# Gate and up weights read as chunks of 2 k-blocks x 1024 columns instead of 4 x 512

## What is computed

```python
def swiglu(h, wg, wu, wd):
    return (jax.nn.silu(h @ wg) * (h @ wu)) @ wd

def moe_swiglu(h, w_router, wg, wu, wd):
    ...
    logits = (xt @ w_router).astype(jnp.float32)
    top_v, top_i = lax.top_k(logits, TOP_K)
    gates = jax.nn.softmax(top_v, axis=-1)
    gate = jnp.sum(jax.nn.one_hot(top_i, N_EXPERTS, dtype=jnp.float32) * gates[..., None], axis=1)
    y = jnp.zeros_like(xt)
    for e in range(N_EXPERTS):
        y = y + gate[:, e:e + 1].astype(xt.dtype) * swiglu(xt, wg[e], wu[e], wd[e])
    return y.reshape(B, S, D)
```

## Time and profile before

| | us |
|---|---|
| median of 3 runs | 1585.43 |
| lowest and highest | 1585.12, 1586.38 |
| profiled execution, its own time | 1585.69 |
| its span | 1583.9 |
| of it before the first pair's first matmul | 669 |
| first pair | 669 to 894 |
| second, third and fourth pair | 894 to 1117, 1117 to 1342, 1342 to 1567 |

### The profile page before, as it was taken

One profiled execution on the slowest core, in us unless ns is written; L12 is line 12 of the kernel. 1 busy time (PEld: TensorE's weight loads), 2 busy tenths in 40 slices (PEclk: granted clock), 3 DMA queues, 4 the chain that ended last, 5 costly groups with the idle time before them and its releaser, 6 DMA issues.

```text
span 1583.9 us, 20830 instructions
## 1 busy us (share of the span) xinstructions
PE 1523.3 (96%) x7379; PEld 1259.0 (79%) x7379; DVE 1285.2 (81%) x1555; ACT 1104.4 (70%) x1475; POOL 118.7 (7%) x242
## 2 busy tenths in 40 slices
PE   6999999999999999699999999999999999999995
PEld 5788788888888888588887788788787887787784
DVE  5686585566545556689999999999999999999998
ACT  3664564645434364278888888888888888788886
POOL 3433431101000010100000000000000000000000
PEclk9999999999999999699999999999999999999998
DMA  9545444535545554369999999999999999999995
GB/s 330 202 156 173 156 158 135 182 116 186 173 146 198 193 179 160 136 230 372 391 397 406 393 385 387 387 406 407 385 386 387 391 408 400 384 387 386 399 407 224
DMA packets 203364, 462.70 MB, mean 292 GB/s; under 512 B 7934, under 2 KB 12428, under 8 KB 203132
## 3 DMA queue, kind: packets, MB, share of 16 engines
q1 hardware_dynamic: 200304, 453.80, 78.5%
q0 software_dynamic: 1904, 5.38, 1.3%
q10 hardware_dynamic: 1052, 2.19, 0.4%
HBM read 460.29 MB, written 1.05 MB: 291 GB/s over the span
## 4 chain that ended last, share of the span: by engine, by line
PE 67%; DMA 13%; DVE 12%; issue 3%; ACT 2%; DVEq 2%; SPq 0%; ACTq 0%
PE ps L2138 8%; PE ps L2139 8%; PE ps L2140 8%; DVE wlo_sb L1378 8%; DMA raw_sb<-moe_wu 7%; PE ps L2595 6%; PE ps L2597 6%; PE ps L2596 6%; PE ps L2610 5%; PE ps L2611 5%; DMA raw_sb<-moe_wg 2%; DMA raw_sb<-moe_wd 2%; ACT whi_sb L998 2%; DMA raw_sb<-w_in 2%; PE ps L2556 2%
## 5 line engine op out<-in xcount | busy, mean ns | idle before, releaser
L1378 DVE TENSOR_TENSOR wlo_sb<-raw_sb,whi_sb 128x1024 fp32r<-128x1024 f32 x662 | 772.6, 1219 | 44.8 <-ACT whi_sb L998 42.1
L998 ACT ACTIVATE whi_sb<-raw_sb 128x1024 fp32r<-128x1024 f32 x662 | 661.3, 1053 | 137.9 <-PE ps L2597 69.5
L1370 DVE TENSOR_TENSOR wlo_sb<-raw_sb,whi_sb 128x1024 fp32r<-128x1024 f32 (+2 forms) x198 | 230.1, 1203 | 146.1 <-ACT whi_sb L990 145.1
L990 ACT ACTIVATE whi_sb<-raw_sb 128x1024 fp32r<-128x1024 f32 (+2 forms) x198 | 192.3, 1023 | 163.3 <-PE ps L2140 131.8
L2138 PE MATMUL ps<-whi_sb,xlo_sb 128*128 128x512 f32 (+2 forms) x544 | 212.8, 391 | 4.4 <-DVE xlo_sb L1417 4.2
L2139 PE MATMUL ps<-wlo_sb,xhi_sb 128*128 128x512 f32 (+2 forms) x544 | 208.5, 383 | 0.0
L2140 PE MATMUL ps<-whi_sb,xhi_sb 128*128 128x512 f32 (+2 forms) x544 | 208.4, 383 | 0.0
L2595 PE MATMUL ps<-whi_sb,xlo_sb 128*128 128x512 f32 x448 | 181.5, 405 | 5.7 <-DVE wlo_sb L1378 4.4
L2610 PE MATMUL ps<-whi_sb,xhi_sb 128*128 128x512 f32 x448 | 177.8, 397 | 2.2 <-DVE wlo_sb L1378 2.1
L2597 PE MATMUL ps<-whi_sb,xhi_sb 128*128 128x512 f32 x448 | 175.4, 391 | 0.0
L2611 PE MATMUL ps<-wlo_sb,xhi_sb 128*128 128x512 f32 x448 | 175.0, 391 | 0.0
(11 more groups left out here) (394 smaller groups left out, 2129.2 us busy)
## 6 DMA issues: line engine op xcount, KB each, us to landing
raw_sb<-moe_wg SPq DMA_DIRECT2D x113, 1024.0 KB, 11.3
raw_sb<-moe_wd SPq DMA_DIRECT2D x112, 1024.0 KB, 10.9
raw_sb<-moe_wu SPq DMA_DIRECT2D x109, 1024.0 KB, 11.9
raw_sb<-w_in SPq DMA_DIRECT2D x40, 1024.0 KB, 5.2
raw_sb<-w_out SPq DMA_DIRECT2D x16, 1024.0 KB, 5.0
raw_sb<-ffn_wg SPq DMA_DIRECT2D x10, 1024.0 KB, 5.1
raw_sb<-ffn_wu SPq DMA_DIRECT2D x10, 1024.0 KB, 5.1
raw_sb<-ffn_wd SPq DMA_DIRECT2D x10, 1024.0 KB, 5.1
```

Of the source, the lines that this page charges most:

```text
L990: nc.scalar.activation(whi[i % SPLIT][:, c:c + k // 2, 0:n], raw[i % RAW][:, c:c + k // 2, 0:n], ACT.Copy).then_inc(hi_ready, 1)
L998: nc.scalar.activation(whi[i % SPLIT][:, c:c + KC // 2, :], moe_raw(i, l)[:, c:c + KC // 2, :], ACT.Copy).then_inc(hi_ready, 1)
L1370: op = V.tensor_tensor(wlo[i % SPLIT][:, c:c + k // 2, 0:n], raw[i % RAW][:, c:c + k // 2, 0:n], whi[i % SPLIT][:, c:c + k // 2, 0:n], ALU ...
L1378: op = V.tensor_tensor(wlo[i % SPLIT][:, c:c + KC // 2, :], moe_raw(i, l)[:, c:c + KC // 2, :], whi[i % SPLIT][:, c:c + KC // 2, :], ALU.s ...
```

## The change

It alters `job_chunks` and all that reads it. The 7 blocks become three groups of two blocks (1024 columns) and one single block (`GROUPS` = 4). A group is 4 gate chunks and then 4 up chunks of 2 k-blocks x 1024 columns; the seventh block stays at 4 x 512. The number of chunks, their bytes, the steps of a pair, `FIRST_ORDER` and `PAIR_ORDER` are as before.

- Gate of a group fills both banks of its job (`bank_of`), and up of the group fills the same two. The first up chunk waits for the reading of gate: for H half by half (`heavy_bank_free`), for L at once (`light_waits`). The first gate chunk of the next group waits for the reading of up.
- Within a gate or up chunk PE runs the first half of columns through and then the second (`order_of`). PE tells of the end of the first half with the new semaphore `h_half_ps`.
- ACT reads H's gate as two `Silu` of 512 columns, and DVE makes H's product as two of 512. L's reading, L's folds, `Silu`, product and splits, and H's turn and split, are done once for a group with twice the width.
- `act_h` moves into the unused half of `xlo`. `gate_l` and `value_l` become one buffer `row_l` of 1024 columns.

```diff
 def job_chunks():
-    up = [Chunk(which, p * NC, NC, k0, KC, p, k0 == 0, k0 + KC == KT)
-          for p in range(BLOCKS) for which in "gu" for k0 in range(0, KT, KC)]
+    up = [Chunk(which, q * WIDE, WIDE, k0, WIDE_K, q, k0 == 0, k0 + WIDE_K == KT)
+          for q in range(WIDE_BLOCKS) for which in "gu" for k0 in range(0, KT, WIDE_K)]
+    up += [Chunk(which, WIDE_BLOCKS * WIDE, NC, k0, KC, WIDE_BLOCKS, k0 == 0, k0 + KC == KT)
+           for which in "gu" for k0 in range(0, KT, KC)]
...
@@ scalar_program, pair; act_hi_moe(act, i + SPLIT, j) stands ahead of it in both @@
                     if i in plan.gate[HEAVY_JOB]:
-                        p = plan.gate[HEAVY_JOB][i]
-                        act.wait_ge(split_used, number(AT_MOE, i + 1, PER, j))
-                        if not first(j) or p:
-                            act.wait_ge(hT_ps, done + p)
-                        nc.scalar.activation(act_h[:, :], acc[:, HEAVY_JOB, 0, :], ACT.Silu).then_inc(hg_silu, 1)
+                        q = plan.gate[HEAVY_JOB][i]
+                        if not first(j) or q:
+                            act.wait_ge(hT_ps, done + q)
+                        for p in blocks_of(q):
+                            if p % 2 == 0 and q < WIDE_BLOCKS:
+                                act.wait_ge(h_half_ps, 2 * WIDE_BLOCKS * j + 2 * q + 1)
+                            else:
+                                act.wait_ge(split_used, number(AT_MOE, i + 1, PER, j))
+                            nc.scalar.activation(act_h_of(p), in_blocks(h_bank(p, "g")), ACT.Silu).then_inc(hg_silu, 1)
...
                     if i in plan.gate[LIGHT_JOB]:
...
-                        nc.scalar.activation(gate_l[:, :], acc[:, LIGHT_JOB, 0, :], ACT.Copy).then_inc(lg_copied, 1)
+                        nc.scalar.activation(row_l[:, 0:NC * len(blocks_of(q))], l_banks(q, "g"),
+                                             ACT.Copy).then_inc(lg_copied, 1)
...
+            def heavy_bank_free(chunk, j, h):
+
+                q = chunk.block
+                if chunk.which == "u" and chunk.n == WIDE:
+                    pe.wait_ge(hg_silu, BLOCKS * j + 2 * q + h + 1)
+                elif q:
+                    pe.wait_ge(h_act, BLOCKS * j + 2 * (q - 1) + bank_of(chunk, h) + 1)
+                elif h == 0 and not first(j):
+                    pe.wait_ge(yg_lo, 4 * j)
...
@@ light_waits @@
+                elif chunk.first and chunk.which == "u" and chunk.n == WIDE:
+                    pe.wait_ge(lg_copied, done + q + 1)
+                elif chunk.first and q:
+                    pe.wait_ge(lu_copied, done + q)
```

More of the change, by code:

```diff
@@ L434, in build @@
         ahead_in_ahi2 = sb("ahead_in_ahi2", [PART, KC, NC], stack=ahead)
-        sb("below_alo2", [PART, NC + below], stack=ahead)
+        sb("below_alo2", [PART, below], stack=ahead)
         ahead_in_alo2 = sb("ahead_in_alo2", [PART, KC, NC], stack=ahead)
@@ new lines, in pair @@
+                    if i in plan.gate[LIGHT_JOB]:
+                        q = plan.gate[LIGHT_JOB][i]
+                        act.wait_ge(split_used, number(AT_MOE, i + 1, PER, j))
+                        if not first(j) or q:
+                            act.wait_ge(luT_ps, done + q)
+                        nc.scalar.activation(row_l[:, 0:NC * len(blocks_of(q))], l_banks(q, "g"),
+                                             ACT.Copy).then_inc(lg_copied, 1)
+                    if i in plan.silu_l:
+                        q = plan.silu_l[i]
+                        act.wait_ge(lgT_ps, done + q + 1)
+                        if not first(j) or q:
+                            act.wait_ge(l_lo, done + q)
+                        nc.scalar.activation(l_act_of(q), l_tp(q, "g"), ACT.Silu).then_inc(l_silu, 1)
@@ L2590, in heavy_step @@
                         hi, lo = x_lhs(k, HEAVY_JOB)
+                        if c == 0 and chunk.first:
+                            heavy_bank_free(chunk, j, h)
                     first, last = chunk.first and c == 0, chunk.last and c == chunk.k - 1
[L2592 to L2597, removed]
+                    o = acc[:, HEAVY_JOB, bank_of(chunk, h), :]
+                    w = c * (chunk.n // NC) + h
+                    mm(o, lo, whi[i % SPLIT][:, w, :], start=first, stop=False)
+                    mm(o, hi, wlo[i % SPLIT][:, w, :], start=False, stop=False)
+                    op = mm(o, hi, whi[i % SPLIT][:, w, :], start=False, stop=last)
+                    if chunk.which != "d" and chunk.n == WIDE and last and h == 0:
+                        op.then_inc(h_half_ps, 1)
                 op.then_inc(split_used, 1)
             def light_step(i, chunk):
-                out = acc[:, LIGHT_JOB]
-                for c in range(chunk.k):
+                for c, h in order_of(chunk):
                     k = chunk.k0 + c
@@ L2606, in light_step @@
                     first, last = chunk.first and c == 0, chunk.last and c == chunk.k - 1
-                    for h in range(chunk.n // NC):
-                        o = out[:, h if chunk.which == "d" else "gu".index(chunk.which), :]
-                        w = c * (chunk.n // NC) + h
-                        mm(o, both, whi[i % SPLIT][:, w, :], start=first, stop=False)
-                        op = mm(o, both, wlo[i % SPLIT][:, w, :], start=False, stop=last)
-                op.then_inc(split_used, 1)
+                    o = acc[:, LIGHT_JOB, bank_of(chunk, h), :]
@@ new lines, in light_step @@
+                    w = c * (chunk.n // NC) + h
+                    mm(o, both, whi[i % SPLIT][:, w, :], start=first, stop=False)
+                    op = mm(o, both, wlo[i % SPLIT][:, w, :], start=False, stop=last)
+                op.then_inc(split_used, 1)
+            def heavy_bank_free(chunk, j, h):
[6 more added lines that the diff above has]
+                    pe.wait_ge(yg_lo, 4 * j)
@@ L2614, in heavy_waits @@
             def heavy_waits(chunk, j):
[L2616 removed]
                 if chunk.which == "d":
                     if chunk.first:
[L2619 to L2626 removed]
+                        pe.wait_ge(hg_silu, BLOCKS * (j + 1))
@@ L2649, in fold @@
+            def fold(q, which):
+                out = l_tp(q, which)
+                for a in range(NC * len(blocks_of(q)) // PART):
+                    at = a % (NC // PART) * LIGHT
+                    op = mm(out[:, a // (NC // PART), at:at + LIGHT], row_l[:, a * PART:(a + 1) * PART], C("fold"), start=True,
                             stop=True)
```

216 lines of the change are left out of this document (114 added, 102 removed).

## The result

The changed kernel takes 1612.4 us (median of four, 1609.1 to 1615.3) against 1585.3 us: 1.017 times as long, 95% interval 1.015 to 1.019. A second set of runs (`after_again`) gave 1609.8 against 1586.2 us, 1.015 (1.014 to 1.017). Predicted were 1598.5 us, 1583 to 1609: the direction is right, the loss is half of the real one, and the median lies outside the range. The profiled execution took 1609.1 us, 23.4 more than that of before.

A forecast was written before the change was run, and what follows sets the result against it. PE was taken as nearly as full as the DMA, so new waits cost time: 1585.7 us profiled, +9.0 in the first pair, +4.2 in three later ones, 1598.9; stated as 1598.5 us, range 1583 to 1609.

The forecast's parts named there:

- longer rows: Gate and up transfers: 192 wide chunks, each 0.147 us quicker, 28 us; only 3.0 us a later pair counted as gain.
- Step 4 of the first pair: H's turn from gate to up: PE waits 2.94 us plus 1.28 for the Silu table's load, 4.2 us.
- Step 12: First pair, H's turn at steps 11 to 12: PE waits 2.94 less a gather of 0.87, 2.1 us.
- Two H turns of a later pair: Gate to up of H: PE waits 1.1 us a turn for ACT's reading, which stands behind a copy.
- the first turn of a later pair: DVE is behind anyway and PE waits for `wlo`, so only 0.7 of 2.1 us was counted.
- L's turns: PE waits for L's reading of gate: 0.8 us a turn in later pairs, 2.5 in all in the first.
- Fewer bursts: Folds and transposes in 12 bursts a pair instead of 21, 0.12 us saved each: 1.1 us less a pair.
- ACT and DVE save some calls too; both have idle time behind PE.: On ACT and DVE: fewer calls from merged work, and idle time behind PE; no size given.
- The tail makes up 1.5 us: End of the first pair, L's steps paced by DVE: a late PE makes up 1.5 us, between 0 and 2.8.
- The clock: PE's clock falls to half behind the waits at steps 4 and 12 of the first pair: +2 to +4 us.
- costs more: Rival: rows stay at 386 GB/s (+9 us) or PE's clock falls in the new waits; 1602 to 1611 us, chance 0.20.
- GB/s near 408 in gate and up when DMA is full: Sign expected in the changed kernel's trace: gate and up transfers near 408 GB/s, with the queue held up by PE.

The follow-up runs named there:

- b_wide: The kernel before with only its gate and up transfers drawn as rows of 4 KB, computation unchanged: 1571.5 us, 0.991 of before.
- a_read_first: The changed kernel with ACT reading the accumulators before it makes the copy for step i+3: 1593.5 us, 1.004 of before.
- a_table: The changed kernel with a dummy Silu on ACT behind the copy for step 3 of the first pair, loading the table there: 1607.1 us.
- a_lumps: The changed kernel with ACT's readings first, the early table load and most of DVE's work per group left out (output not valid): 1582.6 us.
- a_narrow: The changed kernel with only its gate and up transfers drawn as rows of 2 KB, as before the change: 1608.7 us.
- a_both_narrow: The changed kernel with ACT's readings first, the early table load and gate and up transfers in rows of 2 KB: 1592.3 us.
- a_pool_s: The changed kernel with ACT's readings first, the early table load and L's subtraction moved from DVE to POOL: 1598.0 us.
- a_both: The changed kernel with ACT's readings first and the Silu table loaded early by a dummy Silu: 1591.6 us.

## Why the prediction was wrong by half

**The frame was right.** PE, not the DMA, sets the time; the 28 us of "longer rows" don't exist; what PE can gain from them was put at 3.0 us a later pair and is 3.7 to 4.2 (`b_wide`). The place of the loss, ACT's copy ahead of the reading, is confirmed by `a_read_first`: 16 to 19 us hang on it.

**Terms that held.** Step 4 of the first pair: 4.2 said, 4.3 measured, the table's load in it 1.28 and 1.42 (`a_table`). Step 12: 2.1 and 2.0. Step 28: 1.1 and 1.1. Two H turns of a later pair: 2.2 and 1.2 + 0.9. Step 8: 1.1 and 0.9. The 0.7 us put for the first turn of a later pair also came out, at steps 7 and 8, but by luck: it is not the turn (see below).

**Terms that were too high.** L's turns: 1.6 a later pair and 2.5 in the first; measured 0.75 and 0.86. In the second pair L's reading ends at the 6.4 us that I had, but H's own wait makes PE's H step end at 6.0 instead of 5.7; in the third pair the reading ends at 6.1.

**Terms that failed.**
- *Fewer bursts, -1.1 us in each pair.* It is about zero. A fold of 16 small matmuls delays PE by 1.70 us and two of 8 by 0.81 each, eight transposes 0.80 and twice four 0.70: merged bursts cost 0.08 to 0.1 us more apiece, 0.7 to 0.8 a pair, and that is what the fewer late first matmuls save. I took the one from a row and not the other. 4.4 us in all.
- *"ACT and DVE save some calls too; both have idle time behind PE."* This is the step that failed most. With 97 of 100 us busy in gate and up, DVE has no idle time that counts. Its work per group now comes in pieces twice as long: H's product makes PE wait 0.47 us three times a later pair (0.2 forecast, from the start of the product in the earlier trace rows, where the subtraction ahead of it was over earlier) and 0.4, 1.0 and 0.5 us at steps 20, 36 and 44 of the first pair, where I had nothing. Waits for `wlo` appear at steps 22 and 38, and at four steps of the first pair (1.2 us). `a_lumps` gives back 2.1 to 2.6 us a pair of it, nearly all from the waits for `wlo`. Together this is about 7 us. The sum was 10 us short (23.4 against 13.2): these 7, 4.4 for the bursts and 1.7 for the clock, less 4 that L's turns had too much.
- *The tail makes up 1.5 us.* At step 82 nothing: PE's wait is 2.8 us in both. It is no lateness of chunks but DVE adding the scattered results (2.47 us in one piece), which waits for PE's own scatter and moves with it. What does come back is 0.9 us at step 69, a wait that the prediction doesn't name.
- *The clock.* Named as a rival at +2 to +4 us and not put into the sum. Both places named, step 4 and step 12, had the fall: 3.4 us at half, 1.7 lost each time. Net of the fall of before, at the end of the pair, that is 1.7 us in the profiled execution.

**The sum again.** First pair, measured: 12.1 us of new waits in it and 0.5 ahead of the next pair's first matmul, 1.7 of clock, 1.2 in late matmuls and larger bursts, less 0.9 at step 69: 14.6. The second pair: H turns 2.15, L turns 0.75, H's product 1.4, `wlo` at steps 7 and 8 0.7, `wlo` later 0.6, late matmuls and larger bursts 0.9, less 2.6 for late chunks that no longer are and 0.3 at the scatter: 3.6.

**A fold that hid in a wait.** PE's wait at step 7 of a later pair is 1.4 us instead of 0.6 in all variants of the new computation. The second pair, ahead of step 7, before and after:

```profile
912.69 0.60 PE L2683 MATMUL ps<-con_sb,pick_sb 128*128 128x128 f32 x4
913.13 1.00 PE L2648 MATMUL ps<-con_moe_sb,gate_l_sb 128*128 128x64 f32 x8
914.67 0.50 PE L2610 MATMUL ps<-whi_sb,xhi_sb 128*128 128x512 f32 x1 [0.54 <-DVE wlo_sb L1378]
```

```profile
926.96 0.60 PE L2754 MATMUL ps<-con_sb,pick_sb 128*128 128x128 f32 x4
928.90 0.50 PE L2670 MATMUL ps<-whi_sb,xhi_sb 128*128 128x512 f32 x1 [1.34 <-DVE wlo_sb L1423]
```

Step 7 starts no later for it: step 6 is 4.84 us long in both, and in the third pair step 7 starts 21.5 us into the pair in both. Before, L's fold of block 0, 0.81 us, stood in this wait and cost nothing. Now L's first fold is due only when the group's gate is complete, at a place where PE is busy. The longer wait is the sign of work that has moved out of it.

**The rival "costs more"** (1602 to 1611) came nearest in time (1609.8 and 1612.4) and had a small part of the reason: the clock yes, the rows no. That the rows move no faster was wrong as a fact (402 GB/s), and its +9 us are not what was lost either: with short rows the changed kernel takes no longer (`a_narrow`), nor does it without the turn waits (`a_both_narrow`). That its sum comes near is luck. The sign given as proof, "GB/s near 408 in gate and up when DMA is full", could not show, for the DMA was never full.
The Trainium skill, "SBUF — State Buffer", section "SBUF: two separate sides", says that DVE with two SBUF inputs and a GpSimd instruction that reads SBUF exclude each other for a whole instruction. `a_pool_s` agrees: 1.22 us became 2.32 beside POOL's 1.54.

**What stays open.** What else stands between `a_lumps` and `b_wide`. That the wait for H's product can be shortened is not shown: in `a_lumps` it stayed. And no complete kernel here beats the one before. `b_wide` shows 13.6 us of room, but to compute what the text says it needs gate and up of a job in banks of their own at 1024 columns, four for each job, and the transposes have the other four. That wasn't tried.

## What to carry to other kernels

Ask of a faster transfer what PE would wait for without it, and of a new wait which old one it replaces: either can be worth everything alone and nothing together. When a buffer is reused at once, the instruction that frees it has to stand first in its engine's order, and its price is what stands ahead of it, not its own length. Work that is merged into larger pieces is not the same work on an engine that is 97% busy: price each piece at the place where the ring of buffers has least slack, and ask whether a small piece used to fill a wait.

## What was not expected of the hardware

- DVE and POOL take turns: a 128x1024 subtraction of two SBUF operands took 2.32 us instead of 1.22 in each of the 12 cases with POOL's full subtraction beside it. POOL's own 128x512 took 1.5 us.
- The clock fell behind pauses of PE of 2.0 (at step 12), 2.9 and 4.3 us in the first pair, and not behind 1.6; nor behind one of 2.2 us near the end of `a_table`. Behind the 3.0 us at the pair's end it fell in 11 of 14 profiled executions, not in the other three, though the pause was the same. Time and clock go together over the changed kernel's 1607 to 1615 us, where the longer runs have the lower mean clock (0.979 against 0.986), while `a_both`, which has none of the early pauses, stays within 1591.1 to 1592.7.
- Rows of 4 KB, 14 KB apart, moved 402 GB/s (`b_wide`) and rows of 2 KB 386 (before), from one queue with 1 MB a transfer.
